# A decoder layer with product-key experts: the second top-16 step over 100 pairs instead of 256, in 20 segments

## The reference, cut to what matters

```python
q = (xt @ w_query).reshape(t, PEER_HEADS, 2, D_HALF)            # 8 heads, two halves
scores = jnp.einsum('thpd,hpnd->thpn', q, sub_keys)             # 128 keys for each half
sv, si = lax.top_k(scores, PEER_TOPK)                           # top 16 of each half
cand_s = (sv[:, :, 0, :, None] + sv[:, :, 1, None, :]).reshape(t, PEER_HEADS, 256)
cand_i = (si[:, :, 0, :, None] * N_KEYS + si[:, :, 1, None, :]).reshape(t, PEER_HEADS, 256)
top_s, pos = lax.top_k(cand_s, PEER_TOPK)                       # top 16 of the 256 sums
idx = jnp.take_along_axis(cand_i, pos, axis=-1)
gate = jax.nn.softmax(top_s, axis=-1)
a = jnp.einsum('ted,td->te', jnp.take(expert_u, ii, axis=0), xi)
w = gi * jax.nn.gelu(a, approximate=False)
out = jnp.einsum('te,ted->td', w, jnp.take(expert_v, ii, axis=0))
```

## Time and profile before

| | us |
|---|---|
| median of 3 runs | 1636.77 (1636.56 to 1642.16) |
| profiled execution, device time | 1639.41 |
| its span | 1637.70 |
| PE busy in the span | 1569.1 (96%) |
| DVE busy | 1254.9 (77%) |
| ACT busy | 700.8 (43%) |
| POOL busy | 395.4 (24%) |
| mean DMA rate | 260 GB/s |

### The profile page before, as it was taken

The page is one execution under the profiler, slowest core; times in us unless marked ns, Lnnn a source line. Parts: engine busy times, 40 slices in busy tenths (PEclk is TensorE's granted clock), DMA queues, the critical chain, the costliest instruction groups (busy, mean ns, idle before and its releaser), DMA issues.

```text
span 1637.7 us, 23168 instructions
## 1 busy us (share of the span) xinstructions
PE 1569.1 (96%) x7853; PEld 1340.8 (82%) x7853; DVE 1254.9 (77%) x2251; ACT 700.8 (43%) x1286; POOL 395.4 (24%) x326
## 2 busy tenths in 40 slices
PE   5999889999999998999999999899999999999996
PEld 5887755445599998999999999798888888888885
DVE  5778643299759888798789978458888887888888
ACT  3513543212368733785258833233333333333333
POOL 1003300001023300132003357113343333333430
PEclk9799999999999999999999999899999999999998
DMA  9775700001169954799448999969999999999992
GB/s 319 271 260 167 271 12 0 1 1 52 52 223 373 368 210 141 263 359 355 155 149 316 358 415 412 388 230 347 365 342 351 366 351 334 340 359 356 348 324 97
DMA packets 173062, 425.78 MB, mean 260 GB/s; under 512 B 13357, under 2 KB 62509, under 8 KB 169785
## 3 DMA queue, kind: packets, MB, share of 16 engines
q1 hardware_dynamic: 86688, 265.37, 43.7%
q0 software_dynamic: 36864, 134.23, 22.4%
q10 hardware_dynamic: 49432, 25.19, 5.4%
HBM read 372.32 MB, written 52.43 MB: 259 GB/s over the span
## 4 chain that ended last, share of the span: by engine, by line
PE 86%; DVE 6%; DMA 4%; ACT 1%; issue 1%; ACTq 1%; POOL 1%; SPq 0%; DVEq 0%
PE bank L1249 10%; PE bank L1250 10%; PE bank L1253 10%; PE bank L1194 10%; PE bank L1195 10%; PE bank L1196 10%; PE bank L1138 7%; PE bank L1209 5%; PE bank L1121 3%; PE bank L1058 1%; PE bank L1060 1%; PE bank L1059 1%; DMA weights<-in_expert_v 1%; PE bank L996 1%; DVE u_lo L1610 1%
## 5 line engine op out<-in xcount | busy, mean ns | idle before, releaser
L1194 PE MATMUL bank<-h_hi,u_hi 128*128 128x384 f32 x1024 | 350.7, 342 | 21.3 <-DVE u_lo L1610 13.2
L1195 PE MATMUL bank<-h_lo,u_hi 128*128 128x384 f32 x1024 | 345.4, 337 | 0.0
L1196 PE MATMUL bank<-h_hi,u_lo 128*128 128x384 f32 x1024 | 345.3, 337 | 0.0
L1249 PE MATMUL bank<-v_hi,w_hi 128*128 128x512 f32 x768 | 299.4, 390 | 1.4 <-DVE w_lo L1717 1.2
L1250 PE MATMUL bank<-v_lo,w_hi 128*128 128x512 f32 x768 | 298.9, 389 | 0.0
L940 ACT ACTIVATE v_hi<-weights 128x1024 fp32r<-128x1024 f32 x128 | 135.8, 1061 | 331.8 <-PE bank L1253 270.3
L1253 PE MATMUL bank<-v_hi,w_lo 128*128 128x512 f32 x768 | 236.4, 389 | 0.0
L1713 DVE TENSOR_TENSOR v_lo<-weights,v_hi 128x1024 fp32r<-128x1024 f32 x128 | 157.7, 1232 | 95.7 <-ACT v_hi L940 93.8
L1610 DVE TENSOR_TENSOR u_lo<-weights,u_hi 128x1024 fp32r<-128x1024 f32 x128 | 156.0, 1223 | 96.0 <-PE bank L1196 73.6
L1194 PEld LDWEIGHTS bank<-h_hi,u_hi 128*128 128x128 f32 x1024 | 194.8, 190 | 24.6 <-DVE u_lo L1610 12.8
L1195 PEld LDWEIGHTS bank<-h_lo,u_hi 128*128 128x128 f32 x1024 | 194.7, 190 | 0.0
(11 more groups left out here) (280 smaller groups left out, 2324.1 us busy)
## 6 DMA issues: line engine op xcount, KB each, us to landing
weights<-in_uT SPq DMA_DIRECT2D x128, 512.0 KB
weights<-in_expert_v SPq DMA_DIRECT2D x128, 512.0 KB, 5.1
gates_dense<-weights SPq DMA_DIRECT2D x24, 1024.0 KB
weights<-gates_dense ACTq DMA_DIRECT2D x16, 1536.0 KB
shared<-gelu_dense SPq DMA_DIRECT2D x64, 384.0 KB, 8.6
shared<-in_w_ada SPq DMA_DIRECT2D x16, 1024.0 KB, 5.2
gelu_dense<-weights SPq DMA_DIRECT2D x32, 384.0 KB
gelu_dense<-ada SPq DMA_DIRECT2D x32, 384.0 KB
```

The source lines that it names most:

```text
L1194: nc.tensor.matmul(a, uh[:, k, :], h2_hi[:, :, k, :], start=(k == 0), stop=False)
L1195: nc.tensor.matmul(a, uh[:, k, :], h2_lo[:, :, k, :], start=False, stop=False)
L1196: ins = nc.tensor.matmul(a, ul[:, k, :], h2_hi[:, :, k, :], start=False, stop=(k == KC - 1))
L1249: nc.tensor.matmul(acc, wh, v_hi[:, r % 2, cols], start=begin, stop=False)
```

## The change

The sums are taken for 100 pairs: rows a = 0 to 2 with all 16 b (48), rows a = 3 to 15 with b = 0 to 3 (52). This takes two additions in place of one, and the MAX, MAX_INDEX and MATCH_REPLACE run over 100 columns in place of 256. Since a position is no longer a times 16 plus b, the key of the first half is summed up from steps (is_ge against the first position of each row), and b is taken by a mask and a correction. `top16` and `mark` yield more often: 20 segments in place of 11. In the selections of tiles 2 and 3 one product stands behind each of the first 18 segments and none behind the last two, and five of them have a dot. So bodies 12 to 15 have 12, 12, 10 and 0 dots. `u_lo` and one gelu output buffer are placed elsewhere, and at the start of the products `u_lo` of block 0 is written ahead of the last `h2_lo`.

```diff
-SEGMENTS = 11
-BESIDE = {1: (0,) * 10 + (3,), 2: (2, 1, 2, 1, 2, 1, 2, 2, 2, 2, 1), 3: (2, 1, 2, 1, 2, 1, 2, 2, 2, 2, 1)}
+SEGMENTS = 20
+BEST_READY = 16
+BESIDE = {1: (0,) * 19 + (3,), 2: (1,) * 18 + (0, 0), 3: (1,) * 18 + (0, 0)}
...
+DOTS_AT_SEGMENTS = (2, 5, 8, 11, 14)
+DOTS_PER_BODY = {12: 12, 13: 12, 14: 10}
...
+FULL_ROWS, SHORT_ROW = 3, 4
+PAIRS = FULL_ROWS * TOPK + (TOPK - FULL_ROWS) * SHORT_ROW
+def first_pair(a):
+    return TOPK * a if a <= FULL_ROWS else TOPK * FULL_ROWS + SHORT_ROW * (a - FULL_ROWS)
...
-EARLY_SEGMENTS = 6
+EARLY_SEGMENTS = 10
...
-        u_lo = nc.alloc_sbuf_tensor_at("u_lo", [P, LOW, D], F32R, offset=ada_at)
+        u_lo = nc.alloc_sbuf_tensor_at("u_lo", [P, LOW, D], F32R, offset=ada_at + 4 * 3 * D)
...
-                link(tt(cand.rearrange("p h (a b) -> p h a b", b=TOPK),
-                        halves_v[:, :, 0, :].unsqueeze(3).broadcast_to([P, PH, TOPK, TOPK]),
-                        halves_v[:, :, 1, :].unsqueeze(2).broadcast_to([P, PH, TOPK, TOPK]), ALU.add))
+                full = FULL_ROWS * TOPK
+                tt(cand[:, :, 0:full].rearrange("p h (a b) -> p h a b", b=TOPK), ..., ALU.add)
+                link(tt(cand[:, :, full:PAIRS].rearrange("p h (a b) -> p h a b", b=SHORT_ROW), ..., ALU.add))
+                yield
...
-                link(ts(pos_u.bitcast(U32), flat_p, 4, None, ALU.logical_shift_right))
-                link(nc.vector.tensor_copy(pos_a, pos_u.bitcast(U32)))
-                link(ts(pos_u.bitcast(U32), flat_p, 15, None, ALU.bitwise_and))
+                link(nc.vector.tensor_copy(pos, flat_p))
+                link(ts(pos_u.bitcast(U32), flat_p, TOPK - 1, None, ALU.bitwise_and))
                 link(nc.vector.tensor_copy(pos_b, pos_u.bitcast(U32)))
+                link(ts(pos_u.bitcast(U32), flat_p, TOPK - SHORT_ROW, None, ALU.bitwise_and))
+                link(nc.vector.tensor_copy(sel_j, pos_u.bitcast(U32)))
+                link(stt(out=sel_j, in0=pos, scalar=float(full), in1=sel_j, op0=ALU.is_ge, op1=ALU.mult))
+                link(tt(pos_b, pos_b, sel_j, ALU.subtract))
...
+                steps_of_a = halves_v[:, :, 0, 1:TOPK]
+                link(tt(steps_of_a, numbers[:, :, 0, 1:TOPK], numbers[:, :, 0, 0:TOPK - 1], ALU.subtract))
...
                     for a in range(TOPK):
+                        if a == TOPK // 2:
+                            yield
...
                     if n == 1 and segment == SEGMENTS - 1:
+                        rest_of_u(0, 0, True)
                         rest_of_h2(2)
-                        wait_full(dve, "score", NT - 1, 3)
-                        rest_of_u(0, 0, True)
...
+                    if n > 1 and segment in DOTS_AT_SEGMENTS:
+                        next_dot()
...
-            with dve.Fori(LOOP_AT, FEW_DOTS_AT) as I:
+            for I in range(LOOP_AT, ITERS - 1):
                 for r in range(BODY):
                     loop_product(I, r)
-                    for q in range(2):
-                        loop_dot(DOTS_IN_CHUNKS - 2 * BODY * LOOP_AT, 2 * I, 2 * r + q)
+                    for _ in range(DOTS_PER_BODY[I] * (r + 1) // BODY - DOTS_PER_BODY[I] * r // BODY):
+                        next_dot()
```

More of the change, by code:

```diff
@@ L1479, in top16 @@
             def top16(values_out, index_out, rows, groups):
[L1482 to L1496, removed]
-                    ins = nc.vector.max_index(index_out[:, g, 8:16], values_out[:, g, 8:16], rows[:, g, :])
-                link(ins)
+                for half in (slice(0, 8), slice(8, 16)):
+                    for g in range(groups):
+                        ins = nc.vector.max(values_out[:, g, half], rows[:, g, :])
+                    link(ins)
+                    yield
+                    for g in range(groups):
+                        ins = nc.vector.max_index(index_out[:, g, half], values_out[:, g, half], rows[:, g, :])
+                    link(ins)
+                    if half.start:
+                        return
+                    yield
+                    for g in range(groups):
+                        ins = nc.vector.match_replace(rows[:, g, :], values_out[:, g, half], rows[:, g, :], TAKEN)
+                    link(ins)
+                    yield
             def retrieve(n):
                 cand = cand_of(n)
-                pos_a, pos_b, sel_i, sel_j, pos_u = picks(n)
+                pos, pos_b, sel_i, sel_j, pos_u = picks(n)
                 for pair in QUERY_PAIRS:
@@ L1535, in mark @@
                 def mark(s):
                     for a in range(TOPK):
-                        ins = stt(out=marks[:, :, :, a], in0=(pos_a, pos_b)[s].rearrange("p (h k) -> p h k", h=PH), scalar=float(a),
-                                  in1=numbers[:, :, s, a:a + 1].broadcast_to([P, PH, TOPK]), op0=ALU.is_equal, op1=ALU.mult)
+                        if a == TOPK // 2:
+                            yield
+                        if s:
+                            number, at, op = numbers[:, :, 1, a:a + 1], float(a), ALU.is_equal
+                        else:
+                            number, at, op = steps_of_a[:, :, a - 1:a] if a else numbers[:, :, 0, 0:1], float(first_pair(a)), ALU.is_ge
@@ L1539, in mark @@
+                        ins = stt(out=marks[:, :, :, a], in0=(pos, pos_b)[s].rearrange("p (h k) -> p h k", h=PH), scalar=at,
+                                  in1=number.broadcast_to([P, PH, TOPK]), op0=op, op1=ALU.mult)
                     link(ins)
                     link(nc.vector.tensor_reduce((sel_i, sel_j)[s].rearrange("p (h k) -> p h k", h=PH), marks, AX_X, ALU.add))
-                mark(0)
+                yield from mark(0)
                 yield
-                mark(1)
+                yield from mark(1)
@@ L1629, in _, with next_dot @@
             m, dots = 0, 0
+            def next_dot():
+                nonlocal dots
+                dve.wait_ge(gathered[dots % ROWS], 16 * (dots // ROWS + 1))
+                dot(dots, dots)
+                dots += 1
             for n in range(1, NT):
@@ L1669, in loop_product @@
                     rest_of_u(I + 1, 0)
-            def loop_dot(before, I, at):
-                dve.wait_ge(gathered[(before + at) % ROWS], 16 * (before // ROWS + I + (before % ROWS + at) // ROWS + 1))
-                dot(BODY * I + before + at, before + at)
             def loop_add(J, r):
```

33 lines of the change are left out of this document (16 added, 17 removed).

## The result

The changed kernel takes 1629.28 us, the median of five runs (1626.87 to 1631.74). The kernel before took 1640.04 us in the five runs it now has (1636.56 to 1642.16). The ratio is 0.9946, with a 95% interval of 0.9929 to 0.9962. The forecast was 1630.1. The gain is 10.8 us by the two medians, 8.9 by the ratio (6.2 to 11.6), and 10.2 by the spans of the two profiled executions (1637.7 and 1627.5 us).

A forecast was written before the change was run, and what follows sets the result against it. PE was taken to bound the kernel, busy 96% of the span, so only its standing or half-clock time could be won. Start +1.5, selections -2.8 and body 14 -5.4 gave -6.7: 1636.8 to 1630.1 us, range 1622 to 1638.5.

The forecast's parts named there:

- The bound and the four places: PE bounds, 96% busy; it stands at the start, twice in the selection of tile 2 (repeated in tile 3), and in body 14.
- the forecast's first part: Priced PE's stops, 3.05, 3.44, 1.40 and 8.10 us, and half clock behind the long ones, 1.7, 1.6 and 2.6 us.
- Start, +1.5: Start of the products: u_lo now ahead of h2_lo, so PE starts later; taken +1.5 us, bounds +1.1 to +2.1.
- Selections, −2.8: Selections of tiles 2 and 3: stops fall from 4.84 to 3.4 us each, clock falling as before; -2.8 us for two.
- straight line: Selections: MAX of eight groups takes 1.64 us for 128 columns and 2.72 for 256, so 1.4 for 100.
- Body 14, −5.4: Body 14: ACT's second g load blocks 11.3 us, PE stop falls 8.1 to 3.7, clock loss 2.6 to 1.6; -5.4 us.
- the rule by which ACT comes free: Body 14: ACT's second g issue comes free when 1761 packets of its own queue are moved.
- rival 1: Body 14: ACT's block stays under the hidden 7.2 us and costs nothing; -10.7 instead of -5.4, 1624.8 us; chance 0.22.
- one of the signs by which the forecast itself had called this part wrong: Body 14: the forecast is wrong if the stop there is as long as before, or gone.
- the reasoning on turns: Body 14: a queue with work gets its turn each time; 1761 turns at 19.3 ns are 34 us; shorter queues' turns fall away.
- Rival 3, the clock stays up behind 2.6 us: Both later selections: the clock does not fall behind the 2.6 us stop; -3.2 us more, 1626.9 us; chance 0.17.

The follow-up runs named there:

- experiment 9: Changed kernel with last h2_lo ahead of u_lo again, two selection products moved to the last two pieces, second g load issued in body 15: 1613.82 us, ratio 0.9862.
- experiment 1: Changed kernel with the start order undone, the last h2_lo back in front of u_lo of block 0: 1627.63 us, ratio 0.9943.
- experiment 5: Changed kernel with its 100 pairs, but the selection products placed as the coarse pieces had them, two or none beside a piece: 1631.22 us, ratio 0.9960.
- experiment 12: The kernel of experiment 1, unchanged, in a second profiled execution on another chip: 1630.37 us, against 1623.19 for the first profiled execution.
- experiment 4: Changed kernel with the dots in their old places, none in the selections and 16, 16, 8 and 4 in bodies 12 to 15: 1634.09 us, ratio 0.9968.
- experiment 7: Changed kernel with 16, 16 and 2 dots in the last three bodies instead of 12, 12 and 10: 1629.65 us, ratio 0.9951.
- experiment 8: Changed kernel with 9, 9 and 16 dots in the last three bodies instead of 12, 12 and 10: 1635.94 us, ratio 0.9986.
- experiment 11: Kernel before, with only ACT's second g load moved from the fifth product of body 14 to the fifth of body 15: 1628.78 us, ratio 0.9954.

## Why the prediction came out right, and which step did not

*The bound and the four places.* Right, but for a small wait in each selection that the forecast left out (0.24 and 0.23 us, at 636.00 and 826.72). By the forecast's first part the selections cost 9.7 us of stops and 3.2 of clock, and body 14 8.1 and 2.6, together 23.6 us. The kernel of experiment 9, in which these are mended and the start is as before, is faster by 1637.97 - 1613.82 = 24.2 us, and its product stage is shorter by 24.0.

*Start, +1.5.* Measured 4.29 against 3.05 us, +1.24, with `h_lo` as the last releaser; experiment 1 takes it back. The products start at 452.04 us and not at 450.9, because the stretch ahead was 1.0 us longer in this execution.

*Selections, −2.8.* The mechanism is right: nothing over 0.3 us in the first 16 pieces, 2.44 us for the gate weights and 0.42 behind the turn where 2.6 and 0.8 were forecast. With the small waits counted on both sides the stops went from 10.2 to 6.3 us, −3.9. The clock fell as assumed, but cost 5.2 us in place of 3.5, so the sum is −2.1. The prices of 100 columns were right too: eight MAX take 1.41 us (experiment 5 shows the row) for 1.4 by the straight line from the earlier trace rows.

*Body 14, −5.4.* Here the step failed: the rule by which ACT comes free. The forecast had ACT released when 1761 packets of its own queue are moved, at equal turns of three queues, and got a block of 11.3 us and a stop of 3.7. In the profile after the block is 5.02 us and the stop is gone, which is rival 1, and one of the signs by which the forecast itself had called this part wrong. The packets refute the rule. Here is ACT's queue from the first g issue to the release of the second, after:

```profile
q10 hardware_dynamic: 2352, 1.20, 19.0%
```

and in experiment 12:

```profile
q10 hardware_dynamic: 2684, 1.37, 16.2%
```

Neither is 1761, and they are not one number. The kernel with the long block had moved more, so the count is no condition of release. The two parts of the reasoning on turns do show. One is that g moves ahead while the other queues are empty: in the 17.5 us between the two issues ACT's queue moved 2018 packets after, against 811 in 17 us before:

```profile
q10 hardware_dynamic: 2018, 1.03, 21.1%
```

By the rule 1761 packets were through before the second issue, and it should not have been held at all; it was held for 5.02 us. Nor does this count tell the short block from the long: in experiment 12 it is 1874. The other part is the equal turns. Once the second load was issued, SP's and ACT's queues moved the same number (after, 1032 to 1045 us):

```profile
q1 hardware_dynamic: 820, 2.89, 56.1%
q10 hardware_dynamic: 815, 0.42, 11.2%
```

On this the Trainium skill, "DMA: Bandwidth & Descriptors", in the section on queues, rings and completion order, says that each DMA engine goes round the queues that have work, a packet at a time. The equal counts agree, for packets of 3.5 KB and of 512 B. The error was to take a rate of turns for a condition of release.

What came in the place of the size: the block has two lengths with the new places of the dots, about 5 and 12.5 us, and which of them an execution gets is not set by the code alone (experiment 12). With the old places it was 15.29 and 14.96 us in the two profiles there are. The forecast of 11.3 lies between, and the profiled execution showed neither its block nor its stop. In that profile body 14 gave 8.10 − 1.66 us of stops and 2.6 of clock, 9.0 us instead of 5.4.

The sum for the product stage is −2.1 − 9.0 = −11.1, against −11.9 measured and −8.2 forecast. With the start (+1.2), the longer stretch ahead of it (+1.0) and the second dense stage (−0.6) it is −9.5, against 10.2 us of span; 0.7 us stays unexplained.

*Luck.* That 1629.28 lies 0.8 us from 1630.1 is luck in part. The forecast takes 6.7 us off a median of three runs, 1636.77; over five runs the kernel before takes 1640.04, 3.3 us more. The gain was 10.8 us by the medians and 8.9 by the ratio, so the forecast had it too small, and the low start made up for it. A mixture of short and long blocks in the runs without a profile would bring the median towards the forecast too, but no run shows it.

*Rival 3, the clock stays up behind 2.6 us.* It did not, in either selection. But the fall is not fixed. The window from 445 to 470 us, behind the start stop of 2.98 us, in the two executions of experiment 1's kernel, the first:

```profile
445.00:470.00 25.00, 22.18 (x120) 22.18 (x121) 9.53 (x11) 11.34 (x17) 2.24 (x2) 0.93 0.41 139
```

and the second (experiment 12):

```profile
445.00:470.00 25.00, 22.30 (x128) 22.05 (x129) 11.25 (x12) 12.95 (x23) 3.76 (x2) 1.00 0.46 159
```

The same stop cost 1.75 us of clock (0.93) in one and nothing (1.00) in the other. "TensorE: Matmul & The Clock Gate" of the Trainium skill says in its part on the clock gate that the judged stretch runs freely and that the result varies from run to run of one kernel; these two rows agree, and so does the 0.93 against 0.86 behind equal stops in the two selections.

*Still open:* what decides between the short and the long block, and what exactly lets ACT go. Experiments 4, 7 and 8 point to the places of the dots (14.96, 10.78 and 0.39 us, none of them a length seen with 12, 12 and 10 dots), but each by one profile only.

## What to carry to other kernels

When a piece of side work makes the main engine wait, price both its largest piece against the slack of one block and its last pieces against the first consumer; here the first needed the finer pieces and the narrower step together, and the second needed two products moved later. When a DMA issue blocks a compute engine, first move the issue to a place where the load before it is through: four lines did as much as the whole change. And do not read a gain or a loss of some us at such a place from one profile; take a second one of the same kernel.

## What the runs showed of the hardware that was not expected

The issue of one DMA from ACT held the engine for 4.64 us in one execution and for 12.89 in another of the same kernel, with PE not stopped and stopped for 6.12 us. The two kernels in which the issue was moved spread over 3.3 and 4.4 us (experiments 9 and 11, four and six runs), the others over 4.9 to 11.3; no run shows that the block is the reason, since the start of the products alone varies by 3.9 us. And the kernel with 0.39 us of block and the first g load in the crowded stretch was slower than one with 5.02 us, because the rows of u came late (experiment 8).
